# A fused query-key weight, paired gate products, a later gate chain and squares summed by GpSimd

## The reference

```
x = x + mlstm_mixer(rmsnorm(x, ml_norm), ...)        # width 2048 inside, 4 heads of 512
    x_in, z = split(h @ w_in)
    xc = silu(causal_conv4(x_in))
    q, k = blockdiag(xc, w_q), blockdiag(xc, w_k)    # blocks of 4 x 4
    v    = blockdiag(x_in, w_v)
    gates = [q, k, v] @ w_if + b_if                  # input and forget gate of each head
    scores = (q @ k^T) / sqrt(512) * decay(gates)    # causal, summed and normalised
    y = (norm(scores @ v) * ln_w + skip * xc) * silu(z);   out = y @ w_out
x = x + nsa_mixer(rmsnorm(x, nsa_norm), ...)
x = rmsnorm(x, final_norm)
second block: x + mixer(rmsnorm(x, norm_mix)); x + ffn(rmsnorm(x, norm_ffn));
              x + sigmoid(rmsnorm(x, norm_ple) @ w_gate) * (p @ w_proj); rmsnorm(x, norm_final)
rmsnorm(x, g) = x * rsqrt(mean(x * x) + 1e-6) * g
```

## Time and profile before

| what | value |
|---|---|
| median of 3 runs | 2349.63 us (2349.48 to 2350.58) |
| the profiled execution, its own time | 2354.35 us |
| its span, first to last instruction | 2352.4 us |
| mean granted TensorE clock | 0.922 of full speed |
| TensorE matmul busy | 2048.3 us, 87% |
| VectorE, ScalarE, GpSimd busy | 49%, 29%, 12% |

### The profile page before, as it was taken

One profiled execution on the slowest core, in us unless ns is written; L12 is line 12 of the kernel. 1 busy time (PEld: TensorE's weight loads), 2 busy tenths in 40 slices (PEclk: granted clock), 3 DMA queues, 4 the chain that ended last, 5 costly groups with the idle time before them and its releaser, 6 DMA issues. The chain is left out here.

```text
span 2352.4 us, 36449 instructions
## 1 busy us (share of the span) xinstructions
PE 2048.3 (87%) x15648; PEld 1605.5 (68%) x15648; DVE 1154.9 (49%) x1683; ACT 672.4 (29%) x1071; POOL 270.8 (12%) x282
## 2 busy tenths in 40 slices
PE   8998977869999789899999849587586899999997
PEld 7666735538887566688888438476484678888876
DVE  3653344343334477624346874646646444543534
ACT  2223221122212156532211452322222232222232
POOL 2000010020001045300000112213120000000000
PEclk9999988979999699999999869798797999999998
DMA  4223311113332000013330100000004223222211
GB/s 144 92 85 112 135 44 63 45 47 111 140 103 86 19 10 10 29 62 128 123 105 30 39 1 3 1 3 3 2 3 170 81 72 108 90 95 102 91 68 48
DMA packets 40431, 159.01 MB, mean 68 GB/s; under 512 B 4176, under 2 KB 13008, under 8 KB 25680
## 3 DMA queue, kind: packets, MB, share of 16 engines
q1 hardware_dynamic: 26064, 142.01, 17.6%
q10 hardware_dynamic: 14208, 14.68, 1.8%
HBM read 139.90 MB, written 16.78 MB: 67 GB/s over the span
## 5 line engine op out<-in xcount | busy, mean ns | idle before, releaser
L237 PE MATMUL ps<-act_hi,whi 128*128 128x512 f32 x1408 | 566.8, 403 | 42.1 <-PEq L758 16.1
L238 PE MATMUL ps<-act_lo,whi 128*128 128x512 f32 x1408 | 558.1, 396 | 0.0
L239 PE MATMUL ps<-act_hi,wlo 128*128 128x512 f32 x1408 | 557.4, 396 | 0.0
L219 DVE TENSOR_TENSOR wlo<-raw,whi 128x2048 fp32r<-128x2048 f32 (+2 forms) x113 | 250.4, 2216 | 203.9 <-ACT whi L210 203.6
L237 PEld LDWEIGHTS ps<-act_hi,whi 128*128 128x128 f32 x1408 | 270.3, 192 | 115.7 <-issue 53.4
L210 ACT ACTIVATE whi<-raw 128x2048 fp32r<-128x2048 f32 (+2 forms) x113 | 209.0, 1849 | 377.2 <-PE ps L239 219.0
L239 PEld LDWEIGHTS ps<-act_hi,wlo 128*128 128x128 f32 x1408 | 270.3, 192 | 58.0
L238 PEld LDWEIGHTS ps<-act_lo,whi 128*128 128x128 f32 x1408 | 270.5, 192 | 56.6 <-issue 1.4
L2363 PE MATMUL ps<-f_hi,whi 128*128 128x512 f32 x256 | 100.3, 392 | 0.0
L2365 PE MATMUL ps<-f_hi,wlo 128*128 128x512 f32 x256 | 99.7, 389 | 0.0
L2364 PE MATMUL ps<-f_lo,whi 128*128 128x512 f32 x256 | 99.6, 389 | 0.0
(11 more groups left out here) (422 smaller groups left out, 3148.5 us busy)
## 6 DMA issues: line engine op xcount, KB each, us to landing
raw<-stream_in SPq DMA_DIRECT2D x107, 1024.0 KB, 4.9
v_scratch<-v_out ACTq DMA_DIRECT2D x16, 256.0 KB, 2.4
z_scratch<-zt ACTq DMA_DIRECT2D x16, 256.0 KB, 3.9
ml_v<-v_scratch SPq DMA_DIRECT2D x4, 1024.0 KB, 5.0
ml_z<-z_scratch SPq DMA_DIRECT2D x16, 256.0 KB, 2.6
cmp_w<-cmp_w_in SPq DMA_DIRECT2D x2, 2048.0 KB, 9.4
z_scratch<-in_zt ACTq DMA_DIRECT2D x16, 256.0 KB, 4.6
mix_g<-z_scratch SPq DMA_DIRECT2D x16, 256.0 KB, 4.6
```

The costliest lines, as they stand in the source:

```text
L219: dve.tensor_tensor(k.wlo[b % 2][:, 0:n], k.raw[b % RAW_SLOTS][:, 0:n], k.whi[b % 2][:, 0:n].bitcast(F32), ALU.subtract).then_inc(k.lo_don ...
L237: pe.matmul(bank, hi, k.act_hi[:, kt, :], start=(kt == 0), stop=False)
L238: pe.matmul(bank, hi, k.act_lo[:, kt, :], start=False, stop=False)
L239: last = pe.matmul(bank, lo, k.act_hi[:, kt, :], start=False, stop=(kt == rows // P - 1))
```

## The change

1. `stage_open` multiplies the widened query and key weights of each of the 16 feature tiles into one 128 x 128 matrix `k.qk` (16 more matmuls of 128 columns), which ScalarE copies out at the end. The ring is used as if it had six buffers. `stage_ml_heads` makes only k' = qk^T xconv (four matmuls for a head) and takes `xconv` itself as query.
2. The gate products of two tiles are done together, after the odd one, in turn into rows 0 to 35 and 64 to 99 of bank 6. `xin` has four buffers.
3. The gate chain runs while the first output tiles of z are multiplied; it adds the two halves of the gate rows. The transposes come after output tile 7.
4. For five of the six norms (`pooled`) GpSimd adds the eight squares up (`gather`, `gather_last`), and TensorE does the one-column matmuls once, after row block 6. For all norms VectorE runs `mean_squares` after input tile 6 and `spread_diag` after the last.

```diff
 multiply_tile:
-        if norm and kt == 1:
+        if norm and kt == (6 if norm.pooled else 1):
             norm.last_mean(pe)
-        if norm and kt == 7:
-            norm.spread(pe)
     last.then_inc(k.tile_done, 1)
+    if norm:
+        norm.spread(pe)
...
 Norm:
+    def gather(self, pool):
+        for n in range(1, KD - 1):
+            for x in range(self.sets):
+                m = self.sets * n + x
+                pool.wait_ge(self.sq_done, m + 1)
+                if n >= 2:
+                    pool.wait_ge(self.sq_used, m - 2 * self.sets + 1)
+                pool.tensor_tensor(self.total[:, x, :], self.total[:, x, :], self.sq[:, m % 2, :], ALU.add) \
+                    .then_inc(self.sq_used, 1)
+    def gather_last(self, pool):
+        for x in range(self.sets):
+            pool.wait_ge(self.last_sq, x + 1)
+            pool.tensor_tensor(self.total[:, x, :], self.total[:, x, :], self.sq[:, (self.sets * (KD - 1) + x) % 2, :],
+                               ALU.add).then_inc(self.last_add, 1)
     def last_mean(self, pe):
-        self.sums(pe, KD - 1, self.last_sq, 0).then_inc(self.last_sum, 1)
+        if self.pooled:
+            pe.wait_ge(self.last_add, self.sets)
+            for x in range(self.sets):
+                last = self.sums(pe, x, self.total[:, x, :], x == 0, True)
...
     def roots(self, pool):
         pool.memset(exponent, -0.5).then_inc(self.exponent_set, 1)
+        if self.pooled:
+            self.gather_last(pool)
...
     def feed_dve(self, dve):
-            if i == 2:
+            if i == 6:
                 self.mean_squares(dve)
-            if i == 5:
-                self.spread_diag(dve)
+        self.spread_diag(dve)
...
 stage_add (and the same in stage_ffn and stage_ple):
+                norm.gather(pool)
-                if norm and n:
-                    norm.mean(pe, n - 1)
...
 stage_open:
+            for g in range(4):
+                act.wait_ge(qk_mm, g + 1)
+                act.activation(k.qk[:, 4 * g:4 * g + 4].rearrange("p t c -> p (t c)"), k.ps[:, g, :], ACT.Copy)
-                    eng.wait_ge(fold_mm, u - W + 1)
+                    eng.wait_ge(fold_mm, u - W + 3)
+                if m == 1:
+                    last = pe.matmul(k.ps[:, t // 4, t % 4 * P:(t % 4 + 1) * P], wide[:, u % W, :], wide[:, (u - 1) % W, :],
+                                     start=True, stop=True)
...
 stage_ml_inner:
-                    if t >= 2:
-                        dve.wait_ge(gate_mm, t - 1)
+                    if t >= 4:
+                        dve.wait_ge(gate_mm, t // 2 - 1)
-                    pe.matmul(k.ps[0:36, 6, :], k.fold[:, 1, u, :], xin[:, u % 2, CONV - 1:CONV - 1 + S],
-                              start=(u == 0), stop=False)
-                    pe.wait_ge(xconv_ready, u + 1)
-                    pe.matmul(k.ps[0:36, 6, :], k.fold[:, 0, u, :], k.xconv[:, u, :], start=False,
-                              stop=(u == ML_T - 1)).then_inc(gate_mm, 1)
+                    if u % 2:
+                        pe.wait_ge(xconv_ready, u + 1)
+                        for n in (u - 1, u):
+                            pe.matmul(k.ps[0:36, 6, :], k.fold[:, 1, n, :], xin[:, n % 4, CONV - 1:CONV - 1 + S],
+                                      start=(n == 0), stop=(n == ML_T - 1))
+                            last = pe.matmul(k.ps[64:100, 6, :], k.fold[:, 0, n, :], k.xconv[:, n, :], start=(n == 0),
+                                             stop=(n == ML_T - 1))
+                        last.then_inc(gate_mm, 1)
...
 stage_ml_gate: the chain of ScalarE and VectorE moves from ahead of the tile loop into it
+                if t == 2:
+                    gates()              # ScalarE: four reads of bank 6, Abs, Exp, Ln
+                if t == 5:
+                    act.wait_ge(d_step, 10)
+                    act.activation(floor, floor, ACT.Exp, scale=-1.0).then_inc(a_step, 1)
                 if t == 2:
+                    sum_gates()          # VectorE: inp += inp2, fg += fg2
+                if t == 3:
+                    scan_gates()         # VectorE: the chain as before
+                if t == 8:
                     dve.wait_ge(g_tr, 2)
-                if t == 1:
+                if t == 7:               # TensorE: wait, then the transposes
...
 stage_ml_heads:
-                    pe.matmul(k.ps[:, b, :], wide[:, c % 2, 0, :], x, start=True, stop=True)
-                    pe.matmul(k.ps[:, b + 1, :], wide[:, c % 2, 1, :], x, start=True, stop=True).then_inc(s["qk_mm"], 1)
                 pe.matmul(k.ps[:, 6, :], k.const("sel", 512)[0:4, ...], k.neg_m[:], ...)
+                for c in range(TT):
+                    t = TT * (first + h) + c
+                    pe.matmul(k.ps[:, c, :], k.qk[:, t, :], k.xconv[:, t, :], start=True, stop=True).then_inc(s["k_mm"], 1)
-                for c in range(TT):      # ScalarE copies q, VectorE copies k
+                for c in range(0, TT, 2):
+                    act.activation(kk[:, c, :], k.ps[:, c, :], ACT.Copy).then_inc(s["k_act"], 1)
+                for c in range(1, TT, 2):
+                    dve.tensor_copy(kk[:, c, :], k.ps[:, c, :]).then_inc(s["k_dve"], 1)
```

More of the change, by code:

```diff
@@ L271, in squares @@
             m = self.sets * n + x
-            if used and m >= 2:
-                act.wait_ge(used, m - 1)
+            held = self.sets if self.pooled else 0
+            if used and m >= 2 + held:
+                act.wait_ge(used, m - 1 - held)
             scale = self.k.col(self.before, n) if x else 1.0
-            act.activation(self.sq[:, m % 2, :], self.k.xT[:, n, :], ACT.Square, scale=scale).then_inc(done, 1)
+            out = self.total[:, x, :] if self.pooled and n == 0 else self.sq[:, m % 2, :]
@@ L277, in square @@
+            act.activation(out, self.k.xT[:, n, :], ACT.Square, scale=scale).then_inc(done, 1)
     def square(self, act, n):
         self.squares(act, n, self.sq_done, self.sq_used)
-    def sums(self, pe, n, done, count, used=None):
-        for x in range(self.sets):
[L283 to L291, removed]
+    def gather(self, pool):
[7 more added lines that the diff above has]
+                    .then_inc(self.sq_used, 1)
@@ new lines, in gather_last, with sums @@
+    def gather_last(self, pool):
+        for x in range(self.sets):
+            pool.wait_ge(self.last_sq, x + 1)
+            pool.tensor_tensor(self.total[:, x, :], self.total[:, x, :], self.sq[:, (self.sets * (KD - 1) + x) % 2, :],
+                               ALU.add).then_inc(self.last_add, 1)
+    def sums(self, pe, x, src, first, last):
+        for i in range(TT):
+            done = pe.matmul(self.k.ps[:, 7, 4 * x + i:4 * x + i + 1], src[:, i * P:(i + 1) * P],
+                             self.k.const("mean_ones")[:, 0:1], start=(first and i == 0), stop=last, skip_group_check=True)
+        return done
@@ L302, in scale_stage @@
         self.hi_done, self.fed = k.sem(f"{tag}_hi_done"), k.sem(f"{tag}_fed")
-    def gain_of(self, i):
-        return self.both[:, i:i + 1] if self.before else self.k.col(self.gain, i)
+        self.last_add = k.sem(f"{tag}_last_add")
     def last_square(self, act):
@@ L418, in _ @@
                     norm.square(act, n)
+        @block.gpsimd
+        def _(pool):
+            if norm:
+                norm.gather(pool)
         @block.tensor
@@ L2328, in _ @@
             norm.roots(pool)
+            then.gather(pool)
         @block.scalar
@@ L2366, in _ @@
                     last.then_inc(k.tile_done, 1)
-                    if f == 3 and n:
-                        then.mean(pe, n - 1)
         @block.vector
@@ L2456, in _ @@
                 last.then_inc(k.tile_done, 1)
-                if n >= 2:
-                    then.mean(pe, n - 2)
-            then.mean(pe, KD - 2)
         @block.vector
```

154 lines of the change are left out of this document (76 added, 78 removed).

## The result

The changed kernel takes 2324.22 us (median of 4 runs, 2321.64 to 2324.95) beside 2350.11 (4 runs, 2349.48 to 2352.02) for the kernel before on the same chip: a ratio of 0.988, interval 0.9868 to 0.9892. It is faster, by 25.9 us (1.1%); 52.7 were forecast, and 2324 lies above the range of 2280 to 2316. The profiled execution took 2324.95 us (span 2323.1), 29.4 less than that of before.

A forecast was written before the change was run, and what follows sets the result against it. TensorE, busy for 87% of the span, was taken as the bound. Terms 7.4 + 7.5 + 26.8 + 18.3 - 7.3 = 52.7 us, from a median of 2349.63, gave 2297 us; 8-in-10 range 2280 to 2316.

The forecast's parts named there:

- Something in the stages of the other parts: Case of an effect in stages outside the five summed terms; no size given, chance 0.02.
- Low levels everywhere: Rival: new idle gaps each cost a low clock stretch; heads give 18, norms lose 4 more; 2310 us, chance 0.14.
- Opening: Opening stage: 16 added matmuls of 128 columns cost 7.3 us, at TensorE's lower clock level.
- TensorE's clock rises in the opening: Rival: more columns stream, so the opening's loop, means and first output tile run faster; about 2283 us, chance 0.11.
- Inner stage: Pairing gate products of two tiles, column halves working at once, gives 7.4 us; a 2.5 us loss in single file.
- single file: Rival in the inner stage: gate products on two column halves don't overlap; costs 9.9 us, 2307 us, chance 0.10.
- Gate stage: Gate chain beside the first output tiles removes idle time after tile 1; gives 7.5 us, ends 5 and 8.
- Heads: Two heads stages: first head gains 4.4 us, second 9.0, in each; 26.8 us in all, ends 18 and 32.
- Norms: Squares added by GpSimd spare means between tiles, but following stages start later; gives 18.3 us net.
- norm_final: Final part: VectorE's and GpSimd's adds exclude each other; minus 3.0 us, ends plus 2 and minus 6.
- Slower by GpSimd's adds: Rival: 42 GpSimd adds hold up VectorE where TensorE waits, 52.9 us come back; about 2355 us, chance 0.03.

The follow-up runs named there:

- e1_fill: Changed kernel plus eight fp32r matmuls of 128x512 (1.8 us) into an unused bank behind the NSA input stage's last output tile; 2294.9 us.
- e10_onehalf: Changed kernel with eight filling matmuls behind the NSA input stage's last tile, both gate products of a tile in the same column half; 2307.72 us.
- e8_unpooled: Changed kernel with filling matmuls behind the NSA input stage; squares of norms nsa, ffn, ple and final summed by TensorE again; 2300.06 us.
- e2_after_shift: Changed kernel plus eight fp32r matmuls of 128x512 behind output tile 10 of the NSA input stage, the gap staying; 2314.6 us.
- e3_before_shift: Kernel before plus eight fp32r matmuls (1.8 us) behind output tile 10 of the NSA input stage, nothing of the change in it; 2376.42 us.
- e4_before_gap: Kernel before plus two ScalarE copies of 128x512 at the NSA input stage's end, making the gap 3.3 us instead of 2.3; 2374.74 us.
- e5_before_fill: Kernel before plus eight filling matmuls (1.8 us) behind the last output tile of the NSA input stage; 2352.54 us.
- e11_burst: Changed kernel, gap left as it is, plus six fp32 matmuls of 128x512 at the start of the NSA preparation; 2304.32 us.
- e6_order: Changed kernel with filling matmuls behind the NSA input stage; a pair's gate products issued xin both first, then xconv both; 2295.58 us.

## Why the forecast failed, point by point

**The step that failed is the sum's term for the stages of the other parts: nothing.** The sum assumed that they keep their time, with "Something in the stages of the other parts: 0.02". They lost 27.0 us, between tile 64 and tile 77, because the preparation fell to 1.2 GHz at a gap that had been there before. The forecast had the number in hand: the earlier trace rows show such a stretch at 0.50, right behind that stage, and the 2.3 us gap was in the trace. "Low levels everywhere" was the nearest rival, but it priced only gaps that the change makes, at 13 us, and never asked what happens at the old ones. With that one stretch back at 2.4 GHz (e1_fill) the time is 2294.9 us, 2 from the forecast of 2297. Part of that closeness is chance: the inner stage and the heads gave more than was reckoned, below. The Trainium skill (TensorE: Matmul & The Clock Gate, Part 1: The HAM clock gate) says that the count of slow matmuls of one kernel varies from run to run with the phase of the gate at its start, and that the ramp to the high level is worth less than 1% of a typical span. The one execution in 32 of the kernel before at 2372.32 us fits the first. The second speaks of the ramp; a fall in mid-kernel costs more here, 27 of 2323 us, 1.2%, in one place, and the changed kernel's four runs lie within 3.3 us, so it seems that all have it.

**Opening: right.** +7.1 against +7.3. The row of L536 and L533 shows another split than reckoned: an added matmul takes 0.57 us (20.25 to 20.82 for one), and the ones of eight columns 0.38 instead of 0.43. Net it is 0.43 each: the loop takes 27.3 us instead of 20.5. The level did not rise in this stage, as the rival "TensorE's clock rises in the opening" had it: the first record of L237 takes 0.77 us in both kernels.

**Inner stage: mechanism right, size off: -15.3 against -7.4.** Six of the seven pairs gain 1.6 us each (+0.8, then -2.4), 9.6 together, where 1.0 each was reckoned: eight records take 1.75 us instead of 2.15, as both halves start together and no record is left uncovered. The first pair gains 3.0. There the kernel before waits longer for the first `xconv`, ahead of which ScalarE loads a table (1.28 us), and the forecast counted the usual 0.23 for every tile. Timeline, kernel before:

```profile
60.68 1.05 PE L633 MATMUL ps<-xconv,fold 128*36 128x512 f32 x2 [1.65 <-ACT xconv L579]
```

Together the pairs give 12.6, and e1_fill has the same 12.6. The other 2.3 lie in tile 0 (10.8 us before, 8.5 after): the level rose 3.4 us behind the first product instead of 8.2. That is luck, of the same sort as the 27 us with the other sign; in e1_fill tile 0 takes 10.4 us, and its inner stage gives 12.5. The rival "single file" is refuted by e10_onehalf, at 12.8 us (the forecast said 9.9).

**Gate stage: -5.3 against -7.5.** The gap behind tile 1 is gone (5.8, as forecast), the late splits hold. But the level was low from 180.2 to 187.0, behind a wait of 2.69 us for the last `xconv`, and the first tile of the stage lost 2.4. In e1_fill the level is back at 184.2, that tile loses nothing, and the stage gives 7.7. So the forecast's term holds where the level does.

**Heads: -29.6 against -26.8.** First stage 13.2 against 13.4: the first head's scores came 2.8 us sooner than the tiles ahead of them (4.4 reckoned, the products in front of them being partly at 1.2 GHz: eight records in 5.79 us, 3.70 in the second stage), the second head's another 10.4 (9.0). Second stage 16.4: 5.3 and 11.0. There the first head's products run at 2.4 GHz. The mechanism is the one forecast; its low stretches were priced a little too high.

**Norms: -15.1 against -18.3.** The adding stages gave their 0.95 or 1.85 a tile, and the spread came 13.8 us behind the stage's start, to a tenth as forecast. norm_nsa, ffn and ple together gave 10.0 against 11.0; norm_mix 8.6 against 10.3: the 12.0 between its tiles are there, but its spread cost 2.6 instead of 1.7 and its first tile 0.9. In e1_fill all the norms together give 17.7; the difference lies mostly in how long the level is low in the first tiles of these stages. norm_final lost 3.5 against 3.0, for the reason given: L219 beside GpSimd's add, 1.33 us against 0.69 (timelines of e1_fill and e8_unpooled above). The Trainium skill (SBUF — State Buffer, Who interferes with whom) has that rule, and the traces of e1_fill and e8_unpooled agree: without GpSimd's adds L219 takes 0.69 us, and the final part is 3.1 us shorter.

**Slower by GpSimd's adds.** Did not come: L219 keeps its median of 2.29 us in the big blocks.

## What to carry to other kernels

Before an edit that moves a stage in time, list the idle gaps of TensorE of 2 to 3 us that stand ahead of a stage of short matmuls, and what that stage would cost at 1.2 GHz: that sum belongs into the range whether or not the edit touches the stage. A gap of that sort can be closed with a few long matmuls into a bank that nobody reads; here 1.8 us of them bought 29, and as much work put elsewhere bought only 10. And an edit is judged only when the level is the same on both sides: the ratio of 0.988 hid a change worth 55 to 58 us, while the same 1.8 us of harmless work made the kernel before 26 us slower.

## What the runs showed of the hardware

- With the same 2.3 us gap ahead of the same stage, TensorE went on at 2.4 GHz in the traced execution of the kernel before and fell to 1.2 GHz in those of the changed kernel, e2_after_shift and e3_before_shift. What decides between the two was not shown. With 3.3 us it fell (e4_before_gap), with 0.5 it did not (e1_fill, e5_before_fill).
- 54.6 us in which TensorE was busy without a pause, with matmuls of 64x66 and a few of 128x512 in fp32 between them, passed at 1.2 GHz (e3_before_shift, e4_before_gap); the same stage keeps 2.4 GHz if it starts there. In a burst of twelve records of 128x512 the level rose (e11_burst).
- Two fp32 matmuls of 36 columns of weights on different column halves run fully beside each other, 0.43 us a pair of records, whether issued in turn (after) or two and two (e6_order).
- Why the level fell again behind the preparation in every kernel with a fast preparation (785.5 in the kernel before, 740.6 in e1_fill), and what decided the early rise in the changed kernel's inner stage, was not tested.
